# Differential attention on one core: a tile's transposes issued ahead of the branch product beside it, and one rounding copy issued ahead of the output norms

## What is computed

```python
o_b2 = diff_attention(dq, dk, dv, lam, rel_bias)        # 4 heads, 4 blocks of 128 queries
#   logits = q.k * scale + bias, for two halves c of each head
#   p = softmax(logits);  w = p[0] - lam * p[1];  out = w @ v
y_a = o_a @ w_a                                         # branch a, a gated linear attention
o_b2 = merge_heads(rms_norm(o_b2, subn_g) * (1.0 - lam_init))
y_b = o_b2 @ w_b                                        # branch b
merged = sigmoid(gate_a) * y_a + sigmoid(gate_b) * y_b  # gates: h @ w_in, 1024 columns each
return merged @ w_o
```

## Time and profile before

| | |
|---|---|
| median of three runs | 3723.69 us (3720.17 to 3726.69) |
| the profiled execution | 3723.39 us, of which the span of the profile is 3721.7 us |
| TensorE busy | 3159.5 us, 85% of the span |
| VectorE / ScalarE / GpSimd busy | 30% / 26% / 22% |
| loop over the tiles | first layer 278.7 to 438 us, second layer 1456.2 to 1615.6 us |
| `gb` products | first layer 440.7 to 506.8 us, second layer 1618.2 to 1684.4 us |

### The profile page before, as it was taken

How to read it: one execution, slowest core, us unless ns; L and a number is a source line. 1 busy time by engine, 2 the same in 40 slices (tenths; PEclk the granted TensorE clock), 3 DMA queues, 4 the chain that set the end, 5 groups by cost and what they waited for, 6 DMA issues and landing times. The chain is left out here.

```text
span 3721.7 us, 42396 instructions
## 1 busy us (share of the span) xinstructions
PE 3159.5 (85%) x15027; PEld 2046.8 (55%) x15027; DVE 1131.9 (30%) x2001; ACT 962.3 (26%) x1351; POOL 805.8 (22%) x382
## 2 busy tenths in 40 slices
PE   6988987888884798879688777588899998889999
PEld 4764644333332576454433333365688786568877
DVE  4464423111111446431311111134343303434330
ACT  4323311111111522330111111134333323433331
POOL 3311100111111221120011111230243343024432
PEclk7998997899997899889799999789899998989999
DMA  5223332899998122332499999610122331012232
GB/s 209 68 76 126 136 115 91 340 405 409 409 408 311 69 75 99 119 114 92 180 396 408 409 409 407 256 51 31 60 91 80 90 123 51 31 61 91 80 90 69
DMA packets 289710, 663.67 MB, mean 178 GB/s; under 512 B 20190, under 2 KB 114708, under 8 KB 289552
## 3 DMA queue, kind: packets, MB, share of 16 engines
q1 hardware_dynamic: 271680, 623.43, 45.1%
q0 software_dynamic: 17872, 38.14, 2.8%
HBM read 653.64 MB, written 25.69 MB: 183 GB/s over the span
## 5 line engine op out<-in xcount | busy, mean ns | idle before, releaser
L869 PE MATMUL psum<-s_parts 128*128 128x512 f32 (+1 forms) x3744 | 955.2, 407 | 119.5 <-POOL s_parts L757 39.2
L869 PEld LDWEIGHTS psum<-s_parts 128*128 128x128 f32 (+1 forms) x3744 | 723.3, 195 | 327.6 <-issue 85.6
L869 PE MATMUL psum<-s_ring,s_units 128*64 128x512 f32 x3168 | 743.8, 619 | 129.8 <-DMA s_ring<-in_w_expert_in 90.9
L847 POOL TENSOR_TENSOR s_parts<-s_ring,s_parts 128x4096 fp32r<-128x4096 f32 (+2 forms) x52 | 407.8, 7841 | 873.1 <-ACT s_parts L2068 873.1
L869 PEld LDWEIGHTS psum<-s_ring,s_units 128*64 128x64 f32 x3168 | 251.4, 141 | 578.8 <-issue 446.1
L869 PE MATMUL psum<-s_h_low,s_parts 128*128 128x512 f32 (+1 forms) x1872 | 470.7, 392 | 11.2 <-DVE s_hid_low L2039 11.2
L869 PEld LDWEIGHTS psum<-s_h_low,s_parts 128*128 128x128 f32 (+1 forms) x1872 | 350.6, 188 | 96.0 <-DVE s_hid_low L2039 12.1
L869 PE MATMUL psum<-s_units 128*128 (+9 forms) x1520 | 296.5, 412 | 99.1 <-DVE s_gsl L1829 34.3
L757 POOL TENSOR_TENSOR s_parts<-s_ring,s_parts 128x4096 fp32r<-128x4096 f32 (+1 forms) x22 | 180.4, 8200 | 685.0 <-ACT s_parts L2068 685.0
L2068 ACT ACTIVATE s_parts<-s_ring 128x4096 fp32r<-128x4096 f32 (+3 forms) x74 | 237.3, 3209 | 168.4 <-PE psum L869 103.7
L869 PEld LDWEIGHTS psum<-s_units 64*128 64x128 f32 (+3 forms) x1520 | 175.3, 193 | 178.7 <-issue 121.1
(11 more groups left out here) (350 smaller groups left out, 2664.4 us busy)
## 6 DMA issues: line engine op xcount, KB each, us to landing
s_ring<-in_w_expert_in SPq DMA_DIRECT2D x132, 2048.0 KB, 23.5
s_ring<-in_w_expert_out SPq DMA_DIRECT2D x66, 2048.0 KB, 24.6
s_ring<-in_w_in SPq DMA_DIRECT2D x28, 2048.0 KB, 8.8
s_ring<-in_w_ada SPq DMA_DIRECT2D x24, 2048.0 KB, 9.2
s_ring<-in_ffn_w_up SPq DMA_DIRECT2D x40, 1024.0 KB, 6.4
s_ring<-in_ffn_w_down SPq DMA_DIRECT2D x16, 1408.0 KB, 7.0
s_ring<-in_w_out SPq DMA_DIRECT2D x8, 2048.0 KB, 7.8
s_units<-ys_scratch POOLq DMA_DIRECT2D x16, 512.0 KB, 6.4
```

The source lines that it names most:

```text
L847: pool.tensor_tensor(parts[:, s, 0:size], ring[:, s, 0:size], parts[:, 4 + n % 2, 0:size].bitcast(F32), ALU.subtract).then_inc(weights_low ...
L869: return pe.matmul(o, lhsT=lhsT, rhs=rhs, start=start, stop=stop)
```

## The change

In TensorE's program the four transposes of tile i-2 now stand ahead of the branch product of the same turn, and in `order_a()` the two results are swapped too, so that they exchange banks. In ScalarE's program the copy of `T` stands ahead of the copy of `ga`. Behind the loop, `high_part(10)` stands ahead of `head_norms` instead of behind it. No instruction is added or taken away; VectorE's, GpSimd's and SP's programs keep their order.

```diff
--- before.py
+++ after.py
@@ -182,8 +182,8 @@
         if i < len(seq):
             t += [(("L", i, c), "V") for c in range(2)]
         if i >= 2:
+            t += [(("T", i - 2), "A")]
             t += [(branch(i), "A" if branch(i)[0] == "ga" else "V")]
-            t += [(("T", i - 2), "A")]
             if (i - 2) % NT == NT - 1:
                 t += [(("pv", (i - 2) // NT), "A")]
         if late_ada(i):
@@ -1099,6 +1099,11 @@
                         done(mm(o, dq[rows, h, tok(t)], dk[rows, h, :], True, True))
                 if i >= 2:
                     j = i - 2
+                    o = opened(("T", j))
+                    pe.wait_ge(weights_made.sem, weights_made.at(l, j + 1))
+                    for k in range(NT):
+                        last = pe.transpose(o[:, tok(k)], pe_[:, j % 2, 0, tok(k)], ident[:])
+                    done(last)
                     kind, m = branch(i)
                     if kind == "ga":
                         if m % 4 == 0:
@@ -1108,11 +1113,6 @@
                         if m == 0:
                             pe.wait_ge(weights_in_a[RA.slot(("ya",))], RA.landed(l, ("ya",), ("rt",)))
                         fm(("ya", m), slot_view(RA.slot(("ya",)), 4, D), P * m, oa, 4)
-                    o = opened(("T", j))
-                    pe.wait_ge(weights_made.sem, weights_made.at(l, j + 1))
-                    for k in range(NT):
-                        last = pe.transpose(o[:, tok(k)], pe_[:, j % 2, 0, tok(k)], ident[:])
-                    done(last)
                     if j % NT == NT - 1:
                         h = j // NT
                         o = opened(("pv", h))
@@ -2207,15 +2207,15 @@
                     for c in range(2):
                         ae.activation(pe_[:, b, c, :], pe_[:, b, c, :], ACT.Exp, bias=sc[:, 12 + 2 * b + c:13 + 2 * b + c],
                                              accum_out=sc[:, 16 + 2 * b + c:17 + 2 * b + c]).then_inc(exps_made.sem, exps_made.more())
-                if i >= 2 and branch(i)[0] == "ga":
-                    m = branch(i)[1]
-                    copy(mrg[m], done(("ga", m))).then_inc(TA.by(("ga", m)).sem, TA.by(("ga", m)).more())
                 if i >= 2:
                     j = i - 2
                     o = done(("T", j))
                     if j >= NT:
                         ae.wait_ge(TA.done.sem, TA.done_at(l, ("pv", j // NT - 1)))
                     copy(wT[:, :, tok(j % NT)], o.rearrange("p (k s) -> p k s", k=NT)).then_inc(TA.by(("T", j)).sem, TA.by(("T", j)).more())
+                    if branch(i)[0] == "ga":
+                        m = branch(i)[1]
+                        copy(mrg[m], done(("ga", m))).then_inc(TA.by(("ga", m)).sem, TA.by(("ga", m)).more())
                     if j % NT == NT - 1:
                         copy(dq[:, j // NT, :], done(("pv", j // NT))).then_inc(TA.by(("pv", j // NT)).sem, TA.by(("pv", j // NT)).more())
                 if i == 5:
@@ -2231,8 +2231,8 @@
                     high_part(9)
             ae.wait_ge(TA.by(("pv", 3)).sem, TA.freed_at(l, ("pv", 3)))
             ae.wait_ge(TA.done.sem, TA.done_at(l, ("adt", 1)))
+            high_part(10)
             head_norms(norms[12:16], 12, [dq[:, i, :] for i in range(4)], on_temps)
-            high_part(10)
             for m in range(8):
                 ae.activation(gate_b[m], done(("gb", m)), ACT.Sigmoid).then_inc(TA.by(("gb", m)).sem, TA.by(("gb", m)).more())
             squares(KD, lambda k: ae.wait_ge(TA.by(("wo", k)).sem, TA.freed_at(l, ("wo", k))))
```

## The result

| | before | changed |
|---|---|---|
| median | 3721.9 us (4 runs, 3714.9 to 3726.7) | 3671.7 us (4 runs, 3665.6 to 3676.7) |
| ratio | | 0.9866, 95% interval 0.9841 to 0.9890 |
| the profiled execution: span | 3721.7 us | 3663.9 us |

The changed kernel is 50 us faster, where 47 were forecast. The two spans differ by 57.8 us, more than the medians do: the profiled execution of the changed kernel was the fastest of its four.

What follows compares the result with a forecast made beforehand. TensorE, busy 85% of the span, was taken to bound the kernel, idling for GpSimd's low parts and ScalarE's copies. Gains of 11.9 + 11.5 us a layer, twice, make 46.8: 3723.4 to 3676.6 us, range 3662 to 3699.

Steps and rivals of the forecast that it cites:

- pv(0) and pv(2): Value products in turns 5 and 13: waits of 4.37 and 4.36 us and slow running go; gains 7.4 and 5.8 us.
- slow parts: Extra time of TensorE's first matmuls behind idle time: 3.0 us at pv(0), 1.5 at pv(2), 2.5 at pv(1).
- the rival of a loop without gain: Loop waits move elsewhere or modulation transfers set the pace; only the high part's move gains, 3700 us; chance 0.12.
- the slower rival: The weights' chain sets the loop's pace because T(j) blocks the branch product; 3753 us if the chain were 8.0; chance 0.04.
- Turns 8 and 9: GpSimd's hold on VectorE's negation moves to turn 9; T(7) free, pv(1) waits 6.3 us; cost 8.8 against 13.3, gain 4.5.
- the rival 0.14: GpSimd's low part starts before tile 7's last multiply; T(7) waits until 27.5; 2.8 us a layer lost, 3682; chance 0.14.
- T(0): Tile 0's transposes, turn 2: TensorE idle 4.9 us instead of 1.68, slow running 2.0; loss 5.3 us.
- Turns 14 to 17: Loop's end gains nothing, since gb(0) waits for a chain from its weights' issue; 0.5 us added for a slower start.
- gb(4): Behind the loop: released by the sigmoid freeing gb(0)'s bank, 11.0 us earlier, slow start 2.2 instead of 2.7; gain 11.5.
- The sum: 11.9 us a layer from the transposes plus 11.5 from high part 10, 23.4 a layer, 46.8 over two layers.
- the rival in which the clock stays high: New idle times leave TensorE's clock high, up to 8 us a layer more gain; 3661 us; chance 0.08.
- The table load: Before gb(0)'s sigmoid: 1.28 us without draining; the skill's draining of some 1380 ns would make the gain 1.4 us smaller.

Runs made afterwards that it cites:

- the kernel with the transposes alone: Changed kernel with high part 10 put back behind the norms; 3697.2 us against 3723.8 for the kernel before, ratio 0.9931.
- the kernel with the gate weights first: Changed kernel with gb(0)'s weights issued ahead of those of modulation product 11; 3659.2 us against 3719.4 for the kernel before, ratio 0.9830.
- the experiment on turn 2: Changed kernel with ga(0) ahead of T(0) in turn 2 only; 3673.5 us against 3723.8 for the kernel before, ratio 0.9869.

## Why the prediction was right, point by point

- **pv(0) and pv(2).** Waits of 4.4 us and slow parts gone, as counted: the branch product covers the chain. In the kernel with the transposes alone the loop gains as much, so the rival of a loop without gain falls; and T waits for L1696 in no turn but turn 2, so the slower rival does too.
- **Turns 8 and 9.** Right in place and size: T(7) free, pv(1) waiting 6.0 and 6.1 us where 6.3 were counted, with a slow part of 2.6 and 1.7 (2.5). The hold by GpSimd, read from rows of 7.73 and 5.00 us, was shown by two experiments. That it did not also catch tile 7's multiply owes something to luck: the multiply was over 0.16 and 0.26 us ahead of GpSimd's start in the two layers, and 0.05 us ahead in the kernel with the gate weights first. The prediction calls this margin 1 us where it gives the rival 0.14, while its own count, 17.5 against 17.75, leaves 0.25.
- **T(0).** Counted start 290.75 - 278.69 = 12.06 us behind the first score product, measured 12.04 and 12.03. Its slow part was put at 2.0; from T(0) to the next score product it is 8.9 us in the first layer and 7.3 in the second, against 6.1 in the turn after, so 2.8 and 1.2.
- **Turns 14 to 17.** 27.2 us to gb(0) before and after, and an experiment that moves the bound sets them free. The lengthened idle time before gb(0) was put at 0.5 us more of slow start; it cost 1.4 more in the first layer and gained 1.4 in the second.
- **gb(4).** Bank of gb(0) next in line, as counted: 3.35 us of idle time for 3.4. Slow part 1.6 (5.53 - 3.92) instead of 2.2. High part 10 fits ahead of the norms, as counted; GpSimd's low part, the table load and the sigmoid that frees the bank:

```profile
428.34 8.96 POOL L757 TENSOR_TENSOR s_parts<-s_ring,s_parts 128x4096 fp32r<-128x4096 f32 x1
...
457.20 1.28 ACT L2237 ACT_TABLE_LOAD   x1
...
458.49 2.07 ACT L2237 ACTIVATE s_units<-psum 128x512 f32<-128x512 f32 x4
```

- **The sum.** Counted in the loop 12.4 a layer, measured 13.1 and 15.7; behind it 11.5 less 0.5, measured 10.8 and 13.7. The terms that were off most are the slow parts, which I took as one number each and which came out at 0.0 and 2.7 us behind nearly the same idle time (gb(0)). Taken term by term from the rows of both traces they are 3.7 us of the 6.5 between the 46.8 counted and the 53.3 found here: -0.6 in the first layer's loop and 2.0 in the second's, -0.3 and 2.6 behind it. The waits are another 0.8, and the rest, 2.0, is spread over the turns in hundredths of a microsecond. In the first layer these deviations nearly cancel (0.5 us in all), which is luck; the second layer went part of the way to the rival in which the clock stays high. The medians, with 50, cannot tell this from the count.
- **The table load.** The sigmoid starts 1.29 us behind the load's start (457.20, 458.49), and the load 0.02 us behind the end of the last root, so no draining shows beside it, as the row of before had it.

What the prediction did not see is what the experiment on turn 2 showed: it treated the new wait as belonging to ga(0) and T(0) alone.

## What to carry to other kernels

Where a consumer engine must finish with a tile before it can be refilled, issue the short instruction that frees it ahead of the long independent one, and check by the rows that the long one covers the whole round trip; the reordering cost one uncovered round trip where it began, in both places tried here. When a wait goes, look up what is next in line before counting the gain: a bank, a chain of transfers, an instruction held by another engine; these were worth 10, 9 and 26 us here, beside 27 and 23 for the two parts of the change. And count the slow matmuls behind each idle time of TensorE as part of its price, as a range.

## What the runs showed of the hardware

GpSimd's subtraction of two arrays in SBUF holds some VectorE instructions on SBUF until it ends: the negation on 128x2 took 5.76 us beside one of 8.83, and 1.09 us when the same work came in eight pieces; the scaling on 128x512 took 6.11 us instead of 0.49, the multiply 1.63 us instead of 0.75 beside the pieces. VectorE's reductions out of PSUM (0.69 us) and a scalar operation on 128x1 (0.21 us) ran beside it undisturbed. Whether VectorE holds GpSimd in the same way was not tried. In the Trainium skill (SBUF — State Buffer, Who interferes with whom) this is a pair of ports that VectorE and GpSimd share and that one of them holds for a whole instruction; the runs agree for GpSimd's side, and for an instruction of each of two kinds that the section names, the scalar operation and the one with two inputs in SBUF.

The slow start was expected, not its spread. Behind the same idle time (3.62 and 3.57 us) and in one execution, gb(0)'s first 16 matmuls took 6.65 us in one layer and 3.93 in the other. The granted clock tells when it fell (window, length, busy time, PEclk): first the idle time ahead of pv(1), then that ahead of gb(4) and the product behind it, then gb(0) in the first and in the second layer.

```profile
350.40:356.40 6.00, 0.00 (x1) 0.86 0.14 32
...
455.80:459.10 3.30, 0.00 (x0) 1.00 0.78 254
459.10:464.50 5.40, 5.36 (x16) 0.68 0.61 233
...
427.40:433.90 6.50, 6.50 (x17) 0.55 0.08 5
...
1575.20:1578.90 3.70, 3.70 (x16) 1.00 0.16 11
```

Ahead of gb(4) the clock is at its upper level, 2.4 GHz, for the whole idle time, and at the lower one, 1.2 GHz, for a part of the time after TensorE has begun again. Ahead of pv(1) (0.86) and of the first layer's gb(0) (0.86 from 423.8 to 427.4) it fell while TensorE was still idle; ahead of the second layer's gb(0) it did not fall at all. Why the same idle time gives 6.65 us once and 3.93 us once was not tried and stays open.
